# One block's expert output put into x: a rounded part and its remainder in 32 products, or the whole value in 16 full precision products

## The reference

```
def run_block(args):
    xblk, e = args
    return (jax.nn.silu(xblk @ w_gate[e]) * (xblk @ w_up[e])) @ w_down[e]

yb = lax.map(run_block, (xb, blk_e)).reshape(P, D)
out = jax.ops.segment_sum(yb * buf_w[:, None].astype(yb.dtype), buf_tok, num_segments=N + 1)[:N]
```

## Time and profile before

| what | value |
|---|---|
| runs | 1612.6, 1609.94, 1607.69 us; median 1609.94 |
| profiled execution | span 1607.4 us, 2.5 us below the median (it has no time of its own beside the span) |
| PE busy | 1491.0 us, 93% |
| DVE busy | 999.4 us, 62% |
| ACT, POOL busy | 447.4 us, 399.6 us |
| expert stage 0 | about 464 to 912 us, 46 blocks |
| expert stage 1 | about 1139 to 1591 us, 48 blocks |
| link in the stages | 427 to 429 GB/s in nearly all slices |

### The profile page before, as it was taken

How to read it: one execution, slowest core, us unless ns; L and a number is a source line. 1 busy time by engine, 2 the same in 40 slices (tenths; PEclk the granted TensorE clock), 3 DMA queues, 4 the chain that set the end, 5 groups by cost and what they waited for, 6 DMA issues and landing times.

```text
span 1607.4 us, 45636 instructions
## 1 busy us (share of the span) xinstructions
PE 1491.0 (93%) x19098; PEld 980.1 (61%) x19099; DVE 999.4 (62%) x1665; ACT 447.4 (28%) x734; POOL 399.6 (25%) x368
## 2 busy tenths in 40 slices
PE   8999999999989999997789899989999999889996
PEld 6868778687645555554445588667555555445553
DVE  5122112220378888785667889973888877668877
ACT  5242422322432222221112342154122222112222
POOL 4434344244102212111111255112112111111211
PEclk9999999999999999999999999999999999999999
DMA  9212112122289999999999711126399999999995
GB/s 380 106 53 95 63 60 99 53 105 105 85 368 427 429 429 428 429 429 429 427 429 429 336 61 45 55 105 274 123 429 426 429 429 428 429 429 428 428 429 250
DMA packets 33995, 457.63 MB, mean 285 GB/s; under 512 B 3856, under 2 KB 3984, under 8 KB 6544
## 3 DMA queue, kind: packets, MB, share of 16 engines
q1 hardware_dynamic: 33792, 456.57, 68.0%
q10 hardware_dynamic: 144, 0.18, 0.0%
HBM read 454.64 MB, written 2.10 MB: 284 GB/s over the span
## 4 chain that ended last, share of the span: by engine, by line
PE 72%; DMA 21%; DVE 4%; issue 2%; ACT 1%; POOL 0%; DVEq 0%; SPq 0%; ACTq 0%
PE ps L826 14%; DMA hT<-w_down 14%; PE ps L717 10%; PE ps L718 10%; PE ps L719 10%; PE ps L843 8%; PE ps L762 7%; PE ps L809 5%; DMA ring<-w_down 4%; DMA ring<-w_gu 3%; PE ps L991 2%; PE ps L911 2%; PE ps L903 1%; DVE x L1224 1%; PE ps L772 0%
## 5 line engine op out<-in xcount | busy, mean ns | idle before, releaser
L1224 DVE TENSOR_TENSOR x<-x,ps 128x1024 f32<-128x1024 f32 x384 | 451.1, 1216 | 85.8 <-PE ps L809 85.8
L429 POOL TENSOR_TENSOR w_lo<-ring,w_hi 128x512 fp32r<-128x512 f32 x176 | 235.1, 1338 | 384.1 <-ACT w_hi L471 384.0
L452 POOL TENSOR_SCALAR slot_tok<-trig,slot_now 128x512 fp32r<-128x512 f32 x94 | 147.0, 1564 | 711.6 <-PE ps L809 711.6
L826 PE MATMUL ps<-ring,hgT 128*32 128x256 f32 x4160 | 263.3, 395 | 50.6 <-DMA ring<-w_gu 29.7
L826 PEld LDWEIGHTS ps<-ring,hgT 128*32 128x32 f32 x4160 | 130.1, 112 | 151.4 <-issue 44.6
L471 ACT CAST w_hi<-ring 128x512 fp32r<-128x512 f32 x176 | 109.1, 625 | 339.7 <-PE ps L719 339.7
L762 PE MATMUL ps<-area_a,block_rows 128*32 128x256 f32 x3072 | 184.9, 381 | 0.6 <-DVE block_rows L1186 0.6
L545 ACT ACTIVATE y_hi<-ps,slots 128x256 fp32r<-128x256 f32 x94 | 44.8, 476 | 392.8 <-PE ps L843 392.8
L762 PEld LDWEIGHTS ps<-area_a,block_rows 128*32 128x32 f32 x3072 | 101.0, 111 | 69.7 <-issue 5.6
L843 PE MATMUL ps<-ring,aT_e 128*32 128x256 f32 x2080 | 125.7, 382 | 2.7 <-DMA ring<-w_down 2.6
L717 PE MATMUL ps<-w_hi,hT_hi 128*128 128x512 f32 x320 | 125.1, 391 | 3.0 <-DVE hT_lo L1442 1.7
(11 more groups left out here) (234 smaller groups left out, 1921.6 us busy)
## 6 DMA issues: line engine op xcount, KB each, us to landing
ring<-w_gu SPq DMA_DIRECT2D x88, 2048.0 KB, 28.8
ring<-w_down SPq DMA_DIRECT2D x44, 2048.0 KB, 29.8
area_c<-w_gu SPq DMA_DIRECT2D x20, 2048.0 KB, 30.2
area_b<-w_gu SPq DMA_DIRECT2D x20, 2048.0 KB, 32.8
hT<-w_down SPq DMA_DIRECT2D x20, 2048.0 KB, 33.4
ring<-w_pw SPq DMA_DIRECT2D x6, 2048.0 KB, 11.6
ring<-w_v SPq DMA_DIRECT2D x4, 2048.0 KB, 9.1
ring<-w_g SPq DMA_DIRECT2D x4, 2048.0 KB, 8.4
```

What stands on the lines that cost most here:

```text
L429: nc.gpsimd.tensor_tensor(w_lo[:, place, :], ring[:, s, at:at + 512], w_hi[:, place, :].bitcast(F32), ALU.subtract).then_inc(lo_ready, 1)
L452: nc.gpsimd.tensor_scalar(slot_tok[:, :], tok_number, slot_now[:, 0:1], None, ALU.is_equal).then_inc(tok_hot[l], 1)
L826: last = nc.tensor.matmul(ps[32 * g:32 * g + 32, 2, 0:256], hgT[:, n * (KT // 2) + k, :], gate_up[n][:, k, :, g * P:(g + 1) * P], start=(n ...
L1224: return V.tensor_tensor(x[:, i, :].rearrange("p (g c) -> p g c", g=4), x[:, i, :].rearrange("p (g c) -> p g c", g=4), ps[:, bank:bank + 4 ...
```

## The change

The two parts become one: ScalarE writes the scaled output in full precision (`y_out`), VectorE's `y_lo` operation goes, `slot_tok` is plain float32, and each half of the put has 8 full precision products. `y_split` and `y_rounded` become one semaphore, `y_known`, that ScalarE raises.

```
-                    nc.scalar.activation(y_hi[:, :], ps[:, 3, P:P + QW], ACT.Copy,
-                                         scale=slots[:, bass.ds(t + NBLK, 1)]).then_inc(y_rounded[l], 1)
+                    nc.scalar.activation(y_out, ps[:, 3, P:P + QW], ACT.Copy,
+                                         scale=slots[:, bass.ds(t + NBLK, 1)]).then_inc(y_known[l], 1)
...
                 for i in range(2):
                     cols = slice((2 * half + i) * P, (2 * half + i + 1) * P)
-                    for n, part in enumerate((y_hi, y_lo)):
-                        for g in range(4):
-                            rows = slice(32 * g, 32 * g + 32)
-                            last = nc.tensor.matmul(ps[:, bank + g, i * QW:(i + 1) * QW], slot_tok[rows, cols],
-                                                    part[rows, :], start=(i == 0 and n == 0), stop=(i == 1 and n == 1),
-                                                    tile_position=(32 * g, 0))
+                    for g in range(4):
+                        rows = slice(32 * g, 32 * g + 32)
+                        last = nc.tensor.matmul(ps[:, bank + g, i * QW:(i + 1) * QW], slot_tok[rows, cols],
+                                                y_out[rows, :], start=(i == 0), stop=(i == 1),
+                                                tile_position=(32 * g, 0))
...
-                        pe.wait_ge(y_split[l], t + 1)
+                        pe.wait_ge(y_known[l], t + 1)
...
-                    dve.wait_ge(y_rounded[l], t + 1)
-                    V.scalar_tensor_tensor(out=y_lo[:, :], in0=ps[:, 3, P:P + QW],
-                                           scalar=slots[:, bass.ds(t + NBLK, 1)], in1=y_hi[:, :].bitcast(F32),
-                                           op0=ALU.mult, op1=ALU.subtract).then_inc(y_split[l], 1)
```

More of the change, by code:

```diff
@@ L163, in program @@
         block_hot_r = over("block_hot_r", [P, 3, 8, NBLK], area_c_at, route_at)
-        y_hi = over("y_hi", [P, QW], area_c_at, route_at)
-        y_lo = over("y_lo", [P, QW], area_c_at, route_at + QW)
-        slot_tok = over("slot_tok", [P, S], area_c_at, route_at + 2 * QW)
         ident = const[:, C_ID:C_ID + P]
@@ L201, in program @@
         z_squares = area_a[:, :].rearrange("p (c s) -> p c s", c=KT)
+        y_out = area_c[:, route_at:route_at + QW]
+        slot_tok = area_c[:, route_at + QW:route_at + QW + S]
         room = area_c[:, route_at:route_at + 2048]
@@ L267, in program @@
         hot_step, rows_known, pick_mm, staged = (both(n) for n in ("hot_step", "rows_known", "pick_mm", "staged"))
-        slots_hot, slots_spread, tok_loaded, slot_known, tok_hot, y_split, y_rounded, first_mm, second_mm, added = (
-            both(n) for n in ("slots_hot", "slots_spread", "tok_loaded", "slot_known", "tok_hot", "y_split", "y_rounded", "first_mm", "second_mm", "added"))
+        slots_hot, slots_spread, tok_loaded, slot_known, tok_hot, y_known, first_mm, second_mm, added = (
+            both(n) for n in ("slots_hot", "slots_spread", "tok_loaded", "slot_known", "tok_hot", "y_known", "first_mm", "second_mm", "added"))
         gu_half = both("gu_half")
@@ L451, in _ @@
                     pool.nop(nofuse=True)
-                    nc.gpsimd.tensor_scalar(slot_tok[:, :], tok_number, slot_now[:, 0:1], None,
+                    nc.gpsimd.tensor_scalar(slot_tok, tok_number, slot_now[:, 0:1], None,
                                             ALU.is_equal).then_inc(tok_hot[l], 1)
@@ L864, in experts @@
                 total = pe.value_load(cum[0:1, NE:NE + 1], min_val=NE, max_val=NBLK - 1)
-                pe.wait_ge(y_split[l], total + 1)
+                pe.wait_ge(y_known[l], total + 1)
                 pe.wait_ge(tok_hot[l], total + 1)
@@ L1207, in route @@
                 dve.wait_ge(idx_mm[l], 1)
[L1210 to L1213, removed]
+                link.sent(V.tensor_scalar(y_out, const[:, 0:QW], 0.0, None, ALU.mult))
+                link.done(V.tensor_scalar(slot_tok, const[:, 0:S], 0.0, None, ALU.mult))
+                V.sem_inc(y_known[l], 1)
                 V.sem_inc(tok_hot[l], 1)
```

## The result

The changed kernel takes 1626.58 us in the median of 4 runs (1624.14 to 1628.94), the kernel before 1610.86 us (4 runs, 1607.69 to 1612.6). The ratio is 1.0106, 95% interval 1.0089 to 1.0123: slower by 1%. The forecast was 1626 us and slower. A second series gave 1625.04 us and 1.0089 (1.0075 to 1.0104).

A forecast was written before the change was run, and what follows sets the result against it. TensorE and the expert loads were taken as two close limits, waits for loads paying first; 3.3 (stage 0) + 12.7 (stage 1) + 0.6 (last puts) = +16.6 us, giving 1626 us, range 1617 to 1643.

The forecast's parts named there:

- The half of the put: Put on TensorE: each half takes 1.09 us instead of 0.67, 0.42 us more, 0.84 us more per block.
- the bounds: Half of the put: low, paced by its load alone, 0.02 us more; high, full precision loads not hidden, +0.74 us.
- The two nearest rows: Line 826, same length, 0.219 us a group; L967, same shape, eight records in 0.44 us: basis for the half's price.
- The block: A block without waits on TensorE takes 9.37 us instead of 8.53.
- Stage 0: First expert stage: 36.8 us of lateness against the waits, loads catch TensorE near 825.5, stage ends 3.3 us later.
- The reserve of 40 us: PE's waits for loads in stage 0, about 40 us, which a slower block eats first.
- Nine bare blocks: Stage 0 behind the landing of 825.5: nine blocks add 7.6 us, 4.3 us of waits left to eat.
- Stage 1: Second expert stage: 40.3 us added against a reserve of 28, no wait left, taken as +12.7 us.
- each last put: Last put of each stage: both halves on the path, start 0.55 us sooner, +0.3 us per stage.
- VectorE's gain: VectorE loses 0.48 us of work per block, 45 us in all, worth nothing inside the stages.
- the cover of the adds: VectorE's adds end ahead of the next first half; cover 1.0 us, the same before and after.
- The link: Loads in the stages: landings stand still, some 20 us of lateness free, link still above 420 GB/s.

The follow-up runs named there:

- d2: Kernel before with the second part added three times, 32 one-pass products per half of the put instead of 16: 1636.37 us, 1.0158.
- c1: Changed kernel with each full precision product of the put cut into two of 128 columns, twice the weight loads: 1629.75 us, 1.0132 of the kernel before.
- l1: Kernel before with each load of expert weights behind the first three experts halved to 1024 KB: 1549.4 us, 0.9625.
- d1: Kernel before with the second part added twice, 24 one-pass products per half of the put: 1618.96 us, 1.0053.
- d0: Kernel before with the first part alone in the put, 8 one-pass products per half, remainder left out of the output: 1604.94 us, 0.9978.
- v4: Changed kernel with three more VectorE operations (512, 512, 256 columns) per block ahead of the adds behind the second half: 1678.78 us, 1.0428 of the kernel before.
- v1: Changed kernel with one more unused 128x256 VectorE operation per block where the remainder was made before: 1623.21 us, 1.0082 of the kernel before.
- v3: Changed kernel with one more 128x512 VectorE operation per block ahead of the adds behind the second half: 1625.78 us, 1.0102 of the kernel before.

## Why the prediction was right, step by step

**The half of the put.** Forecast 1.09 us, measured 1.08; the bounds had been 0.69 and 1.41. The two nearest rows, one of the same length and one of the same shape, were enough, since they named the same parts: a first load, a pass of 0.219 us per group with 256 columns, the end. d2 and c1 confirm the account from both sides. A dearer weight load did not show: the put's load records have a mean of 185 ns in full precision and 183 ns in `fp32r`.

**The block.** Forecast 9.37 us, measured 9.34.

**Stage 0.** Forecast +3.3 us, measured 450.5 - 447.8 = +2.7 between the first load of gate and up and the last of down. The reserve of 40 us is 41 in l1. The way to the number was not quite the forecast's. The loads catch TensorE again around 825 us, as forecast (landing at 825.5; after: 825.1), but the last catch is later: the wait for `w_down` that I had counted as eaten is still there and ends with the landing at 884.8, on the chain (before: 884.3). What sets the end is that landing, 0.5 us later, and the three blocks behind it, 3 x 0.81 = 2.4 us. Nine bare blocks less 4.3 us of waits happen to give nearly the same.

**Stage 1.** Forecast +12.7 us, measured 466.3 - 452.2 = +14.1. The forecast said that no wait is left and that the landings stand still. Here it was wrong: two waits stand in the trace, 4.1 us together, and the chain still goes through a load, whose landing ends at 1431.7. The same load stands on the chain before:

```profile
1393.58 33.39 DMA hT<-w_down
```

It lands 288.1 us after the stage's first load of gate and up before, and 291.5 us after: 3.4 us later in the stage. The loads did not stand still, because the link carries only 27 GB/s (after: 29) until the first place of the stage is freed and its load issued, and 429 (after: 428) from shortly behind that issue up to this landing. The first issue comes later. Before, then after:

```profile
1158.10 2.72 SPq L308 DMA_DIRECT2D ring<-w_gu  x2
```

```profile
1162.73 3.12 SPq L307 DMA_DIRECT2D ring<-w_gu  x2
```

That is 19.2 and 22.5 us into the stage: two slower blocks, 1.6 us, and 1.6 us of a slower clock in the first block, which is not the put's (next point). Behind the landing the 18 blocks take 174.8 us instead of 164.1, +10.7: 18 x 0.81 = 14.6 less some 3 us of waits that the kernel before has there. So 3.4 + 10.7 = 14.1. Less the 1.6 us of the clock the stage is +12.5. The forecast took one reserve for the whole stage from all 48 blocks, and comes to nearly the same number by another path.

**The ends and what lies between.** Forecast +0.3 us for each last put. Behind stage 1 it is +0.2 (the time from the end of the last down load to the end of the span, 16.5 us against 16.35). The wait for `y_lo` is gone there, and the put starts 0.62 us sooner behind stage 0 (worked out: 0.55), 1.26 instead of 1.88 us after the last down load. In the changed kernel ACT releases it, 0.1 us behind the adds:

```profile
915.73 0.48 ACT area_c L544
916.21 0.12 issue
916.33 1.15 PE ps L807 x16
```

Between the stages I had not seen 1.5 us that the changed kernel is quicker (225.2 against 226.7 us). The transposes and first products behind the last put show the reason in the granted clock. First the kernel before, then the changed one, at the same place:

```profile
916.00:934.00 18.00, 14.80 (x83) 11.73 (x82) 14.16 (x21) 12.50 (x24) 4.72 (x5) 0.91 0.02 9
1138.00:1150.00 12.00, 11.14 (x212) 6.61 (x216) 8.88 (x19) 3.32 (x4) 1.94 (x3) 1.00 0.20 67
```

```profile
919.00:937.00 18.00, 14.74 (x89) 11.55 (x88) 15.41 (x21) 12.50 (x25) 5.96 (x5) 1.00 0.00 1
1139.50:1151.50 12.00, 11.22 (x167) 6.32 (x171) 6.99 (x14) 1.56 (x2) 1.76 (x2) 0.86 0.23 67
```

Before, a stretch at 1.2 GHz falls behind stage 0 (mean 0.91) and none on the start of stage 1 (1.00); after, it is the other way round (1.00 and 0.86). The first block of stage 1 takes 10.8 us instead of 8.4, which is 1.6 more than the put explains. The two cancel in the sum.

It looks as if the change had moved these stretches, but the other runs' traces do not bear that out. Behind stage 0, 0.91 stands also in d1, d2 and l1 (kernel before) and in c1 (changed kernel), and 1.00 also in d0 (kernel before). At the start of stage 1, 0.86 or 0.87 stands in every profile except those of the kernel before and of v4, so also in d0, d1, d2 and l1, whose put is `fp32r`. c1 gives the price of the first: 226.75 us between the stages where the changed kernel has 225.2. So about 1.6 us less in one place and 1.6 us more in the other belong to where the clock fell, and not to the format of the put. Why it falls where it does stays open. That the two cancel is luck.

**The sum.** 0.2 at the start, +2.7, -1.5, +14.1, +0.2: 15.7 us, forecast 16.6. The price of a half and the idea that the waits pay first are shown. That the total is within 1 us is in part luck: both stages came out near their number by another way than forecast, and the clock's two differences cancel.

**VectorE, ScalarE, POOL.** VectorE's gain was forecast at nothing (v1), the cover of the adds at 1.0 us (v3 free with 0.75, v4 bare with 1.95 or more). POOL's `slot_tok` takes 1564 ns in either format.

**The link.** It was to carry on: the two late landings on the chain of stage 0 are within 0.5 us of those before, and issue to landing fell by 9 us of the 20 I had called free. In stage 1 it carries on too, but 3.4 us later.

## What to carry to other kernels

Where two limits lie close together, the cost of a change is not its length times its count: measure the waits of the engine that gets slower, stretch by stretch, and let them pay first; what is left shows where there are none, and behind the last of them. Look also at the first transfer that waits for the slower engine: if the link is idle until then, everything behind it moves. Here 76 us of work cost 16, and 43 us taken away gave 4. An operation removed from an engine that waits becomes idle time on it. And a price that the trace does not show can be built from two rows, one of the same length and one of the same shape, if both give the same account.

No version here beats both kernels with the whole result: the shorter put, which leaves the remainder out, shows that even halving the products gives only 4 us, because of the loads.

## What the runs showed of the hardware

- Four full precision products with 32x128 weights in the four row strips of the array run side by side: a half of four groups with 256 columns takes 1.08 us, which fits 0.22 us a group. The next load of the same strip hides beside the pass: 16 loads take 1.08 us in a half, 32 loads for the same columns 1.10 us.
- Where the put's row tiles follow column tiles, 0.41 us without a weight load stand before it, whatever stands in the put (`fp32r` or full precision, 8 to 32 products) and whatever VectorE does, as long as it is in time. The trace calls it "issue"; no run separates the change of tiles from other causes.
- With fewer waits for loads, TensorE is at 1.2 GHz less: its mean granted clock rises from 0.96 and 0.97 in the late stretches to 0.99 and 1.00. Over the whole span it is 0.982 before and 0.993 after, and 0.976 for the shorter put, where it waits for loads most.
- A mean granted clock of 0.86 over 12 us, or of 0.91 over 18 us, costs about 1.6 us here. Kernels with different puts have it in the same place, and variants of one kernel in different places. Differences of 1 to 2 us between two profiles can be this alone.
